# Sample attention of a decoder step on Trainium2: two sequences side by side, and the first key gathers issued in prompt attention

## The reference, cut to what matters

```python
def _attend_selected(q, k_sel, v_sel, valid):
    ...
    s = jnp.einsum('btngd,btknd->btngk', qg, k_sel).astype(jnp.float32) * HEAD_DIM ** -0.5
    s = jnp.where(valid[:, :, None, None, :], s, -jnp.inf)
    pr = jax.nn.softmax(s, axis=-1).astype(v_sel.dtype)
    o = jnp.einsum('btngk,btknd->btngd', pr, v_sel)
    return o.reshape(b, t, D_ATT)
...
def _dsa_sample(q, k, v, qi, ki, wi, cache_k, cache_v, cache_kidx, page_table):
    ...
    sc = _index_scores(qi, wi, ki_all)
    sc = jnp.where((jnp.arange(n_keys)[None, :] <= tpos[:, None])[None], sc, -jnp.inf)
    _, idx = lax.top_k(sc, n_sel)
    ...
    k_sel = jnp.where(in_past, cache_k[phys, off], k[bidx, nidx])
    v_sel = jnp.where(in_past, cache_v[phys, off], v[bidx, nidx])
    return _attend_selected(q, k_sel, v_sel, valid)
```

## Time and profile before

| | |
|---|---|
| median of three runs | 2883.78 us (2877.87 to 2884.63) |
| profiled execution, span | 2911.0 us |
| TensorE busy, share of the span | 2390.2 us, 82% |
| VectorE busy | 1105.7 us, 38% |
| ScalarE busy | 543.0 us, 19% |
| GpSimd busy | 527.8 us, 18% |

### The profile page before, as it was taken

One profiled execution on the slowest core, in us unless ns is written; L12 is line 12 of the kernel. 1 busy time (PEld: TensorE's weight loads), 2 busy tenths in 40 slices (PEclk: granted clock), 3 DMA queues, 4 the chain that ended last, 5 costly groups with the idle time before them and its releaser, 6 DMA issues. The chain is left out here.

```text
span 2911.0 us, 28942 instructions
## 1 busy us (share of the span) xinstructions
PE 2390.2 (82%) x8116; PEld 1310.8 (45%) x8117; DVE 1105.7 (38%) x2332; ACT 543.0 (19%) x1192; POOL 527.8 (18%) x723
## 2 busy tenths in 40 slices
PE   8799926888176877997898947999999999999960
PEld 1366725532145653443665523444444444444420
DVE  6100064699999972323543501111111111111107
ACT  1200002143133331213211101111111111111112
POOL 1000030010000000000233151232232223223213
PEclk9799966979568788988888968999999999999985
DMA  8600010010000005323113603999887996879963
GB/s 292 228 0 0 0 46 4 5 38 22 0 1 1 1 1 203 147 114 131 65 65 116 207 22 114 304 346 291 271 273 221 287 319 184 277 239 323 317 209 123
DMA packets 214400, 422.84 MB, mean 145 GB/s; under 512 B 20188, under 2 KB 156368, under 8 KB 203417
## 3 DMA queue, kind: packets, MB, share of 16 engines
q1 hardware_dynamic: 181010, 281.80, 28.0%
q0 software_dynamic: 33312, 140.06, 16.8%
HBM read 352.12 MB, written 69.37 MB: 145 GB/s over the span
## 5 line engine op out<-in xcount | busy, mean ns | idle before, releaser
L2686 PE MATMUL psum<-wx,hT_x 128*128 x1424 | 635.7, 600 | 14.2 <-SPq L2567 9.2
L2686 PEld LDWEIGHTS psum<-wx,hT_x 128*128 128x128 f32 x1424 | 265.1, 191 | 374.2 <-issue 374.2
L2723 PE MATMUL psum<-wx,hidT_x 128*128 x712 | 320.5, 593 | 1.6 <-ACT hidT_x L2635 1.6
L2618 DVE COPY hT_x<-psum 128x512 f32<-128x512 f32 x89 | 61.6, 692 | 634.1 <-PE psum L2676 634.1
L2723 PEld LDWEIGHTS psum<-wx,hidT_x 128*128 128x128 f32 x712 | 128.6, 191 | 129.7 <-issue 129.7
L2668 DVE TENSOR_SCALAR y_x<-psum,slot_gate 128x512 f32<-128x512 f32 x89 | 66.8, 751 | 253.6 <-PE psum L2723 201.9
L2608 POOL DMA_INDIRECT scr_acc<-y_x,add_idx x89 | 142.8, 1604 | 43.4 <-issue 43.4
L1541 PE MATMUL psum<-kT,qz_att 128*128 128x512 f32 (+3 forms) x192 | 102.9, 658 | 52.7 <-ACT qz_att L1515 52.7
L2172 PE MATMUL psum<-wo,mixT 128*128 128x512 f32 (+1 forms) x288 | 138.6, 644 | 1.4 <-PEq L1853 1.4
L2635 ACT COPY hidT_x<-psum 128x256 f32<-128x256 f32 x89 | 33.1, 372 | 559.8 <-PE psum L2710 559.8
L1552 PE MATMUL psum<-ident,sm 128*128 128x128 f32 x288 | 56.7, 335 | 85.5 <-ACT pT L1437 49.0
(11 more groups left out here) (536 smaller groups left out, 3323.7 us busy)
## 6 DMA issues: line engine op xcount, KB each, us to landing
wx<-in_w_e SPq DMA_DIRECT2D x192, 1024.0 KB
wa<-in_w_ada SPq DMA_DIRECT2D x12, 2048.0 KB, 8.6
xt<-in_x_prompt SPq DMA_DIRECT2D x16, 512.0 KB, 3.7
w<-in_w_in SPq DMA_DIRECT2D x1, 7440.0 KB
wo<-in_w_out SPq DMA_DIRECT2D x2, 2048.0 KB
scr_x<-x POOLq DMA_DIRECT2D x8, 512.0 KB, 3.0
scr_h<-h POOLq DMA_DIRECT2D x8, 512.0 KB, 3.8
scr_acc<-ysh SPq DMA_DIRECT2D x8, 512.0 KB
```

The costliest lines, as they stand in the source:

```text
L2618: copy(hT[:, par, 4 * half:4 * half + 4], psum[:, half, :].rearrange("p (k c) -> p k c", k=4)).then_inc(done, 1)
L2686: mm = pe.matmul(psum[:, 2 + par, :], hT[:, par, k], wx[:, bass.ds(s, 1), k * 2 * FE:(k + 1) * 2 * FE].rearrange("p o f -> p (o f)"), star ...
L2723: mm = pe.matmul(psum[:, 5 + c, :], hidT[:, k], wx[:, bass.ds(s, 1), at:at + 512].rearrange("p o f -> p (o f)"), start=(k == 0), stop=(k = ...
```

## The change

Sample attention works on pairs of sequences, p = 0 to 3. Sequence 2p has query rows, probabilities and outputs on partitions 0-63, sequence 2p+1 on 64-127 (i = 0 and 1).

- Each chunk of scores has six matmuls, bias, first and second pair of heads, each for i = 0 and then for i = 1. They write partitions 64i to 64i+63 of the same bank. `values(p)` alternates in the same way over the 17 blocks of keys.
- `rep`, `sbias`, `vn` and the block of `prT` for the new keys get 128 partitions, of which POOL fills the new ones with zeros; the stationary operands of bias, scores and values now all have 128 rows and 64 columns.
- Softmax steps have 128 partitions instead of 64; key transposes come in 16 groups a pair, probability transposes are 128 x 128, four to a group, in five groups.
- `kc` is now two separate buffers, one for each i. The first lies in the memory of the index phase's operands (`index_mem`), the second is `kc1`. Gathers of K 0 and 1 are issued on POOL at the start of prompt attention.
- `vc` keeps two buffers, but both belong to the same pair. Gathers go through `gather_pages`: V 0 and 1 after POOL's memsets; then for each pair K of 2p and of 2p+1, each after the transposes of the same buffer in pair p-1, and then, after values(p-1), V of both.
- SP's loads of `vn` wait for its memset; a finished pair is stored with 16 small DMAs.

```diff
@@ prompt attention, POOL
             nc.gpsimd.memset(qz[:], 0.0).then_inc(q_put, 1)
+            for b in range(2):
+                gather_pages(nc, a["cache_k"][0], x["gidx"], b, x["kc"][b].rearrange("p k d -> p (k d)"),
+                             x["k_land"][b])
@@ sample attention, POOL
+            nc.gpsimd.memset(vn[:], 0.0).then_inc(vn_clear, 1)
+            nc.gpsimd.memset(prT[:, PAGES], 0.0).then_inc(pad_made, 1)
             nc.gpsimd.memset(own[:], 1.0).then_inc(own_made, 1)
...
-            for b in range(NB):
-                if b >= 2:
-                    pool.wait_ge(tr_ps, num[("k", b - 2, 7)] + 1)
-                for dst, src, land in ((kc, "cache_k", k_land), (vc, "cache_v", v_land)):
-                    if b >= 2 and src == "cache_v":
-                        pool.wait_ge(o_ps, b - 1)
-                    nc.gpsimd.indirect_dma_start(
...
+            for b in range(2):
+                gather_pages(nc, a["cache_v"][0], x["gidx"], b, vc[:, b].rearrange("p k d -> p (k d)"), v_land[b])
+            for b in range(2, NB):
+                p, i = divmod(b, 2)
+                pool.wait_ge(tr_ps, num[("k", p - 1, 8 * i + 7)] + 1)
+                gather_pages(nc, a["cache_k"][0], x["gidx"], b, kc[i].rearrange("p k d -> p (k d)"), k_land[i])
+                if i == 1:
+                    pool.wait_ge(o_ps, p)
+                    for j in range(2):
+                        gather_pages(nc, a["cache_v"][0], x["gidx"], 2 * p + j,
+                                     vc[:, j].rearrange("p k d -> p (k d)"), v_land[j])
@@ TensorE, values
+                for i in range(2):
+                    pe.wait_ge(v_land[i], 16 * (p + 1))
...
+                    for i in range(2):
+                        rhs = vc[:, i, k] if k < PAGES else vn[:, 2 * p + i]
+                        mm = pe.matmul(psum[64 * i:64 * i + 64, 7, 0:KVH * HD], prT[:, k, 64 * i:64 * i + 64], rhs,
+                                       start=(k == 0), stop=(k == PAGES))
@@ TensorE, scores
+                    for step in range(3):
+                        for i in range(2):
+                            b, m = 2 * p + i, step - 1
+                            if step == 0:
+                                lhs = rep[:, b].rearrange("r h t -> r (h t)")
+                                rhs = bias[:, 4 * c:4 * c + 4] if c < 4 else x["sbias"][:, PAST:]
+                            else:
+                                lhs = qbd[:, m, b]
+                                rhs = kcT[:, i, m, 4 * c:4 * c + 4].rearrange("p k q -> p (k q)") if c < 4 else \
+                                    t["kT"][:, m, SEQ + b * NT:SEQ + (b + 1) * NT]
+                            mm = pe.matmul(psum[64 * i:64 * i + 64, c, 0:w], lhs, rhs,
+                                           start=(step == 0), stop=(step == 2))
                 mm.then_inc(s_ps, 1)
-                if b >= 1:
-                    values(b - 1)
-                pe.wait_ge(p_made, b + 1)
-                for g in groups_of(b):
+                if p >= 1:
+                    values(p - 1)
+                pe.wait_ge(p_made, p + 1)
+                for g in groups_of(p):
                     transposes(g)
```

More of the change, by code:

```diff
@@ L1631, in _ @@
[L1631 to L1634, removed]
-                if b >= 2:
-                    pool.wait_ge(tr_ps, num[("k", b - 2, 7)] + 1)
-                for dst, src, land in ((kc, "cache_k", k_land), (vc, "cache_v", v_land)):
-                    if b >= 2 and src == "cache_v":
-                        pool.wait_ge(o_ps, b - 1)
-                    nc.gpsimd.indirect_dma_start(
[L1641 to L1644, removed]
+            nc.gpsimd.memset(x["sbias"][NS:P, :], 0.0).then_inc(pad_made, 1)
@@ new lines, in _ @@
+            nc.gpsimd.memset(rep[NS:P], 0.0).then_inc(pad_made, 1)
+            pool.wait_ge(pad_made, 3)
+            for i in range(2):
+                half = own[64 * i:64 * i + 64]
+                nc.gpsimd.affine_select(out=half, in_=half, pattern=[[-2 * NT, KVH]], compare_op=ALU.is_ge,
+                                        fill=0.0, base=0, channel_multiplier=1).then_inc(own_made, 1)
+            pool.wait_ge(own_made, 3)
+            for i in range(2):
+                half = own[64 * i:64 * i + 64]
+                nc.gpsimd.affine_select(out=half, in_=half, pattern=[[2 * NT, KVH]], compare_op=ALU.is_ge,
+                                        fill=0.0, base=2 * NT - 1, channel_multiplier=-1).then_inc(own_made, 1)
@@ L1646, in _ @@
         @block.sync
         def _(sp):
+            sp.wait_ge(vn_clear, 1)
             for b in range(NB):
[L1649 to L1654, removed]
+                sp.dma_start(vn[0:NT, b], t["v"][b * NT:(b + 1) * NT, TILES]).then_inc(vn_land, 16)
@@ L1655, in _ @@
+            for p in range(NP):
+                sp.wait_ge(o_made, p + 1)
+                for i in range(2):
+                    b = 2 * p + i
+                    for h in range(HEADS):
+                        sp.dma_start(scr["os"][b * NT:(b + 1) * NT, h * HD:(h + 1) * HD],
+                                     os_[64 * i + h * NT:64 * i + (h + 1) * NT, p % 2]).then_inc(o_out[p % 2], 16)
             for i in range(2):
-                sp.wait_ge(o_out[i], 16 * HEADS * NB // 2)
+                sp.wait_ge(o_out[i], 16 * 2 * HEADS * NP // 2)
@@ L1658, in read_group @@
         def read_group(eng, copy, g, done):
-            kind, b, j = groups[g]
+            kind, p, j = groups[g]
             eng.wait_ge(tr_ps, g + 1)
@@ L1662, in read_group, with groups_of @@
             if kind == "k":
-                if b >= 1:
-                    eng.wait_ge(s_ps, b)
-                copy(kcT[:, :, 2 * j:2 * j + 2].rearrange("p m k q -> p k m q"),
+                if p >= 1:
+                    eng.wait_ge(s_ps, p)
+                i, k = divmod(j, PAGES // 2)
+                copy(kcT[:, i, :, 2 * k:2 * k + 2].rearrange("p m k q -> p k m q"),
                      bank.rearrange("p (k m q) -> p k m q", k=2, m=2)).then_inc(done, 1)
             else:
[L1669 to L1672, removed]
-                else:
[L1674 to L1679, removed]
+                if p >= 1:
+                    eng.wait_ge(o_ps, p)
+                if j < 4:
+                    copy(prT[:, 4 * j:4 * j + 4], bank.rearrange("p (k r) -> p k r", k=4)).then_inc(done, 1)
+                else:
+                    eng.wait_ge(pad_made, 1)
+                    copy(prT[0:NT, PAGES], bank[0:NT, 0:P]).then_inc(done, 1)
+        def groups_of(p):
+            lo = num[("k", p + 1, 0)] if p + 1 < NP else num[("p", p, 0)]
+            return range(lo, num[("p", p, 4)] + 1)
         @block.vector
@@ L1700, in _ @@
-            for b in range(NB + 1):
-                if b >= 1:
-                    if b >= 2:
-                        dve.wait_ge(o_made, b - 1)
-                    dve.wait_ge(p_made, b)
+            dve.wait_ge(own_made, 5)
+            for p in range(NP + 1):
+                if p >= 1:
+                    if p >= 2:
+                        dve.wait_ge(o_made, p - 1)
+                    dve.wait_ge(p_made, p)
                     seq(nc.vector.tensor_reduce(s1[:], s2[:], AX, ALU.add))
```

180 lines of the change are left out of this document (95 added, 85 removed).

## The result

The changed kernel took 2835.3 us (median of four runs, 2830.95 to 2836.36), the kernel before on the same chip 2880.82 (four runs, 2868.92 to 2884.63): ratio 0.984 with a 95% interval of 0.982 to 0.986, 45.5 us less. Forecast were 2847 and a gain of 36.6.

The account below looks back on a forecast made before the run. TensorE's own length was taken to set sample attention. Summing start, two 52.6 us rounds, late last values and tail ended the stage at 1290.9 instead of 1327.8; the 36.9 us gain, scaled to 36.6, gave 2847, range 2832 to 2870.

Parts of the forecast that it names:

- rounds of pairs 1 and 2: Middle rounds of sample attention: each 52.6 us for two sequences, including 19.1 us idle for K gathers, against 53.6 before.
- 2 x 21.2: Time that late K gathers take back in the two middle rounds: each 19.1 us idle plus 2.1 for the cold start.
- Halves overlap: Scores and values of two sequences run side by side on TensorE's column halves, priced at one sequence's length: 12.0 and 7.6 us.
- rival 1: In the scores, the two strided bias streams don't overlap: 16 us more, 2863 us; chance 0.14.
- rival 4: In scores and values the column halves take turns: 77 us more over four pairs, 2924 us; chance 0.06.
- my own lower end of 11.0: Lower bound for a pair's scores: all in parallel and the clean switch between tile shapes saved, 11.0 us.
- the two stretches at half clock: Allowance of 1.6 us in each middle round for the half-clock stretch that scores showed in most rounds before.
- POOL's new memsets: hidden: At the stage's start, POOL's new memsets (vn 1.81 us, the rest smaller, some 5 together) and vn loads end by 1101, hidden.
- rival 2: Key and probability transposes after 19 us idle stay at half clock, as do the first scores: 19 us more, 2866; chance 0.13.
- Rival 3: Late issue of the gathers costs nothing in the two rounds and at the end: some 55 us less, 2792 us; chance 0.05.
- in other words: Recount of the gain: parallel work frees 77 us, other savings some 15; starved starts take 2 x 21.2 and 13.0, tail 3.
- the sum on the span: Step-by-step timeline of sample attention, ending at 1290.9 us where it was 1327.8 before: gain 36.9 us.

Follow-up runs that it names:

- Experiment 1: Changed kernel with the next pair's two K gathers issued on POOL before the wait for values that V stands behind; 2790.47 us.
- experiment 4: Changed kernel with all five score chunks of the left half ahead of all five of the right half; 2873.26 us.
- experiment 7: Changed kernel with POOL's memsets held back until VectorE's set-up has built qbd and rep; 2833.29 us.
- experiment 2: Changed kernel with next K gathers ahead of the wait for values, and V of the last pair put into the key buffers; 2779.52 us.
- experiment 8: Changed kernel with the edits of experiment 2 and experiment 6 together; 2772.86 us.
- experiment 9: Experiment 2's kernel with packed bias reordered by ScalarE, and POOL's memsets but the first held behind VectorE's set-up; 2765.1 us.
- experiment 3: Changed kernel with each chunk's three score matmuls all for the left half, then all for the right; 2834.57 us.
- experiment 6: Changed kernel with the bias stored in page order by VectorE, so TensorE reads it packed, not every 16th element; 2824.09 us.

## Why the prediction held, step by step

The measured 2835.3 lies in the range of 2832 to 2870, but 11.7 us under the forecast, more than the 8 us that it gave as its own error. In the stage 9.5 us are missing.

| step, from the stage's start | forecast us | measured us |
|---|---|---|
| start to scores 0 | 13.3 | 13.7 |
| scores 0 to the end of values 0 | 49.1 | 46.1 |
| rounds of pairs 1 and 2 | 105.2 | 98.1 |
| to the start of values 3 | 13.7 | 13.6 |
| values 3 | 9.7 | 10.3 |
| tail | 9.5 | 9.0 |
| stage | 200.5 | 191.0 |

- *Mechanism.* The pairs halve the work and the gathers' order takes half of that back. The idle times were 18.7, 19.2 and 11.6 us, forecast 19.1, 19.1 and 10 to 11. Experiment 1 shows that the cause is the order and prices it at 41 to 45 us; "2 x 21.2" for the rounds is what it returned (a round 20.3 and 21.5 shorter).
- *Halves overlap* was right, the bias streams included: rival 1 (16 us) is refuted by two bias records in 0.90 us, and rival 4 by experiment 4, which makes the scores take turns and costs 38 us; the forecast's price for them would have been 4 x 11.8 = 47.
- *The term that was mis-sized is the round*, 52.6 forecast, 48.3 and 49.9 measured. Of the 7.1 us in both, 2.4 are the scores, 10.8 for 12.0: I carried the old chunk of 2.86 over, though my own lower end of 11.0 named the saved switch of shapes; experiment 4 shows 2.63 without any overlap. (Scores 0 and 1 have the same 1.2 us too much each, so the scores are 4.8 of the 9.5 us.) And 3.2 are the two stretches at half clock, which I took from the earlier trace rows and which didn't come: the clock is 1.00 over scores 1 and values 0 and over scores 2 and values 1 (second and fourth row of the stretches; the third is a cold start), and so it is over scores 3 and values 2 (1231.9 to 1250.2). Why they stayed away is open; no run varied it alone. In the kernel before, the dip at 1182.4 had gathers beside it (DMA share 1.01), but they aren't enough for one: scores 2 of experiment 1, from 1158.3 to 1169.2, have the same share of 1.01 at a clock of 1.00.
- *"POOL's new memsets: hidden"* was wrong in mechanism. They stretch VectorE's copies to 3.52 us, and TensorE, which I had going on at 1094.3 (3.9 us into the stage), went on 5.8 us into it, after waiting 2.32 for VectorE. It passed unnoticed because the 48 transposes and the last copy then took 7.9 us in place of 9.4: they were not cold to the end. Two errors of 1.9 and 1.5 in opposite directions; experiment 7 shows the first.
- *Transposes and the clock.* After 18.7 us of idle time the granted clock was 0.51 over the first 3.2 us of transposes, and then 1.00: 32 in 5.22 us, the next 32 in 3.66. In experiment 1 it is 1.00 in all of 81 us with 81 transposes at a stretch (line as in rows 1):

```profile
1123.00:1204.00 81.00, 78.87 (x572) 47.25 (x571) 30.62 (x54) 23.71 (x42) 7.50 (x8) 1.00 0.52 209
```
"TensorE: Matmul & The Clock Gate" of the Trainium skill (Part 4, PE-mode transpose) has it that transposes don't bring the full clock; for these float32 transposes both traces contradict it, and rival 2 went with it. By the same page's ratio for column tiles (Part 3, three tiles at 2.38 times one) I had estimated 24.7 us for a pair's scores and values; they take 18.3.
- *Rival 3* (gathers not late, 2792) was the wrong reading of this program. Its price of 55 us, for the two rounds and the end together, is what experiments 1 and 2 returned together (the stage is 55.4 us shorter in experiment 2). That 2792 lies beside the 2790.47 of experiment 1 is chance: that run still has the last wait, and the price was taken off 2847, not off the measured 2835.
- *The sum said twice.* The prediction's recount "in other words" doesn't add up to its gain: 77 + 15 - 42.4 - 13.0 - 3 = 33.6, not 36.9. The forecast rests on the sum on the span, and that one is right.

## What to carry to other kernels

When two units of work are fused into one and a buffer loses its double, read the DMA-issuing queue in program order: whatever stands behind the new wait is late too, and moving two gathers ahead of it was worth nearly as much here as the whole change (43.4 and 46.4 us of the stage). When column halves are fed side by side, interleave them by the step or by the chunk, never by the whole pass. A memset or a strided write put "beside" an engine is free only if neither that engine nor what it feeds is the next one waited for; experiments 7, 8 and 9 each removed a cost and found some or all of it again one step on.

## What the hardware showed that I had not expected

- TensorE starts a record of the right column half ahead of earlier-issued records of the left one: one that was issued behind four of them started with the first (experiment 3, 1104.75). Behind a whole pass of 25 records it starts only with the first of the last four (experiment 4, 1112.48).
- A bf16 moving operand read at every 16th element costs 0.90 us per 512 columns, packed 0.21 (experiment 6). At half clock it costs the same 0.90 (experiment 7, 1104.16 to 1105.06 at 0.50). Two such streams to the two halves take no longer than one: a chunk of both is 2.63 us, as is a chunk of one half in experiment 4.
- POOL's memsets stretch VectorE's eight 64 x 64 float32 copies from 1.21 us to 3.52 (experiment 7); beside one memset alone that ends in their midst they take 1.58 (experiment 9).
- Writing 2048 bf16 elements a partition in a transposed order takes 4.71 us on VectorE and 3.96 on ScalarE, against 0.69 for 2056 packed ones on VectorE (experiments 6 and 9).
